# Two transformer stacks in one launch: heads turned back through a score bank, and the order of work at both borders of the feed-forward stage

## The reference, cut to what matters

```python
def hybrid_layer(x, ...):                       # first block, twice
    proj = rmsnorm(x, norm_g) @ w_in            # 28 columns of 128
    y_a = conformer_conv(a_u, a_v, ...) * silu(a_z)       # 31 taps
    y_b = short_gated_conv(b_b, b_c, b_x, ...) * silu(b_z)
    y_c = window_gqa(c_q, c_k, c_v, swa_sink) * silu(c_z)      # "gqa"
    y_d = neighborhood_attn(d_q, d_k, d_v, na_rpb) * silu(d_z) # "na"
    return x + concat(y_a, y_b, y_c, y_d) @ w_out

def second_block(x, ...):                       # second block, layers l = 0, 1
    proj = rmsnorm(h, attn_norm[l]) @ w_in[l]
    ret = silu(rg) * rmsnorm(retention_chunkwise(rq, rk, rv), ret_norm[l])
    dif = rmsnorm(diff_attention(dq, dk, dv, lam), diff_norm[l]) * (1 - lam_init)
    h = h + concat(ret, dif) @ w_out[l]
    u = rmsnorm(h, ffn_norm[l])
    h = h + (silu(u @ w_gate[l]) * (u @ w_up[l])) @ w_down[l]  # hidden width 2816
```

## Time and profile before

| what | value |
|---|---|
| median of 3 runs | 3571.68 us (3569.9 to 3572.59) |
| the profiled execution | 3570.65 us |
| its span | 3568.0 us |
| mean granted clock of TensorE | 0.988 of full speed |
| busy: TensorE, VectorE, POOL, ScalarE | 96, 55, 38, 28% of the span |
| bytes from and to HBM | 196.94 MB read, 41.68 MB written |

### The profile page before, as it was taken

The page is one execution under the profiler, slowest core; times in us unless marked ns, Lnnn a source line. Parts: engine busy times, 40 slices in busy tenths (PEclk is TensorE's granted clock), DMA queues, the critical chain, the costliest instruction groups (busy, mean ns, idle before and its releaser), DMA issues.

```text
span 3568.0 us, 41967 instructions
## 1 busy us (share of the span) xinstructions
PE 3417.0 (96%) x16504; PEld 2760.4 (77%) x16504; DVE 1960.6 (55%) x2939; ACT 993.6 (28%) x1863; POOL 1353.7 (38%) x592
## 2 busy tenths in 40 slices
PE   8999999999999999898999999999998989999997
PEld 7877778877778888567888888888875778888886
DVE  6668635668636333778656542331447776555324
ACT  2220342130243000554333330110026443333002
POOL 4324214324303433104655634543230255654443
PEclk9999999999999999999999999999999999999998
DMA  4112103112101111102222252211110122223322
GB/s 149 42 48 58 56 19 89 42 30 75 62 13 42 47 42 42 42 7 100 80 86 83 85 192 82 59 48 52 36 60 7 55 94 83 82 84 130 132 81 76
DMA packets 72812, 240.24 MB, mean 67 GB/s; under 512 B 21952, under 2 KB 22336, under 8 KB 66240
## 3 DMA queue, kind: packets, MB, share of 16 engines
q1 hardware_dynamic: 50112, 205.54, 17.2%
q10 hardware_dynamic: 22528, 32.31, 2.8%
HBM read 196.94 MB, written 41.68 MB: 67 GB/s over the span
## 4 chain that ended last, share of the span: by engine, by line
PE 84%; DVE 11%; ACT 2%; issue 2%; DMA 0%; DVEq 0%; ACTq 0%
PE ps L715 48%; PE ps L1102 23%; PE ps L844 3%; DVE st L1876 3%; PE ps L827 2%; PE ps L780 2%; PE ps L798 2%; DVE space_hi L1720 1%; DVE in_lo L1590 1%; DVE st L1596 1%; DVE xt L1578 1%; PE ps L855 1%; ACT st L1221 1%; PE ps L737 1%; DVE sl_r L2194 0%
## 5 line engine op out<-in xcount | busy, mean ns | idle before, releaser
L606 POOL TENSOR_TENSOR w_hi<-w_raw,ones_r 128x1024 fp32r<-128x1024 f32 x182 | 361.8, 1988 | 1775.4 <-PE ps L715 1758.9
L1102 PE MATMUL ps<-sl_r,sl_r 128*128 128x512 f32 x3696 | 843.7, 391 | 22.9 <-issue 22.9
L1102 PEld LDWEIGHTS ps<-sl_r,sl_r 128*128 128x128 f32 x3696 | 696.8, 189 | 168.7 <-issue 23.7
L715 PE MATMUL ps<-in_hi,w_hi 128*128 128x512 f32 x2176 | 696.1, 401 | 37.8 <-DVE in_lo L1590 16.2
L715 PE MATMUL ps<-in_hi,w_lo 128*128 128x512 f32 x2176 | 680.3, 394 | 0.0
L715 PE MATMUL ps<-in_lo,w_hi 128*128 128x512 f32 x2176 | 678.8, 393 | 0.0
L610 POOL TENSOR_TENSOR w_lo<-w_raw,w_hi 128x1024 fp32r<-128x1024 f32 x182 | 505.9, 2780 | 14.3
L715 PEld LDWEIGHTS ps<-in_hi,w_hi 128*128 128x128 f32 x2176 | 394.6, 189 | 143.3 <-issue 56.2
L715 PEld LDWEIGHTS ps<-in_lo,w_hi 128*128 128x128 f32 x2176 | 408.1, 189 | 90.5 <-issue 4.4
L715 PEld LDWEIGHTS ps<-in_hi,w_lo 128*128 128x128 f32 x2176 | 406.5, 189 | 91.9 <-issue 5.8
L715 PE MATMUL ps<-sl_r,w_hi 128*128 128x512 f32 x1408 | 378.7, 391 | 4.7 <-DVE sl_r L2236 4.7
(11 more groups left out here) (206 smaller groups left out, 3423.2 us busy)
## 6 DMA issues: line engine op xcount, KB each, us to landing
w_raw<-w_in SPq DMA_DIRECT2D x184, 512.0 KB, 3.5
raw_pair<-w_ffn SPq DMA_DIRECT2D x44, 1024.0 KB, 4.9
hid_kept<-sl SPq DMA_DIRECT2D x44, 512.0 KB, 2.6
sl<-hid_kept SPq DMA_DIRECT2D x44, 512.0 KB, 7.5
x_put_away<-xt SPq DMA_DIRECT2D x16, 512.0 KB, 7.8
xt<-x_put_away SPq DMA_DIRECT2D x16, 512.0 KB, 6.1
xt<-x_in ACTq DMA_DIRECT2D x8, 512.0 KB, 7.7
space_lo<-c_alibi ACTq DMA_DIRECT2D x2, 2048.0 KB, 7.6
```

The lines of the kernel that those rows point to most:

```text
L606: pool.tensor_tensor(w_hi[:, j, :], w_raw[:, j, :], ones[:, 0:1].broadcast_to([P, KC * P]), ALU.mult).then_inc(pool_own, 1)
L715: last = pe.matmul(ps[:, 2 * j + h, :], w[:, w_slot, (w_k + k) * P:(w_k + k + 1) * P], part[:, k0 + k, h * HALF:(h + 1) * HALF], start=(k ...
L1102: last = pe.matmul(ps[:, to[name], :], ring(sl_r, p, wp[w])[:, k * P:(k + 1) * P], half_of(sl_r, xp[x], k), start=(name in ("P1", "P5") an ...
```

## The change

**Heads.** In "gqa" and "na" the heads are turned back into bank 4, a score bank. The turn waits for the bias of all scores so far in place of bank 6, and the next scores wait for the finish. In "na", VectorE scales the heads ahead of the scores of its step, and ScalarE makes exponentials two steps behind the unit, between its two group copies.

**Border from the projection.** T2 and T3 are built in other banks, so P1 and P5 of pair 0 wait for the low part (T2, 1). The low parts of pair 0's plain weights go from VectorE to POOL (`rest_of_first`), the weights are rounded a step or two earlier on ScalarE, and the first `carry` stands ahead of the last chunk's work.

**Border to the down projection.** The last pair's gate is made in banks 5 and 6, so product 40 waits for the gate before it, and all low parts 1 to 7 are made ahead of the last `hidden`.

```diff
         def op_bank(op, i):
-            return {"T1": (4, 5, 6, 7), "T2": (6, 5, 6, 5), "T3": (7, 4, 7, 4)}[op][i]
+            return {"T1": (4, 5, 6, 7), "T2": (4, 6, 4, 3), "T3": (5, 7, 5, 1)}[op][i]
...
+        def gate_banks(p):
+
+            return (5, 6) if p == HC - 1 else (0, 1)
...
+            def rest_of_first(l, i):
+
+                raw = pair_raw(0)
+                hi, lo, source = ((sl_r[:, RING[0][0], :], sl_r[:, RING[0][4], :], raw[:, HALF:3 * HALF]),
+                                  (ring(sl_r, 0, (1, 0)), ring(sl_r, 0, (1, 1)), raw[:, 3 * HALF:4 * HALF]))[i]
+                pool.wait_ge(pair_hi.handle, pair_hi.at(1, l, rounded_count(0, 2 + i)))
+                pool.tensor_tensor(lo, source, hi.bitcast(F32), ALU.subtract).then_inc(pair_lo.handle, 1)
...
                         sums(l, 0)
+                        rest_of_first(l, 0)
                         sums_lo(l, 0)
+                        rest_of_first(l, 1)
...
+                    if state["back"]:
+                        pe.wait_ge(mixed_out.handle, mixed_out.at(stack, l, state["back"]))
+                        state["back"] = None
...
                     pe.wait_ge(headed.handle, headed.at(stack, l, r0 + n + 1))
-                    bank_6_free()
+                    if kind == "dif":
+                        bank_6_free()
+                        state["free"] = (mixed_out, r0 + n + 1)
+                    else:
+
+                        pe.wait_ge(biased.handle, biased.at(stack, l, p0 + state["p"]))
+                        state["back"] = r0 + n + 1
                     for c in range(4 * width // P):
-                        last = pe.transpose(ps[:, 6, c * P:(c + 1) * P],
+                        last = pe.transpose(ps[:, 6 if kind == "dif" else 4, c * P:(c + 1) * P],
...
-                    to = {"P1": a, "P5": 4 if p else 7, "P6": a, "P2": 0, "P7": a, "P3": 1, "P4": d}
+                    b, c = gate_banks(p)
+                    to = {"P1": a, "P5": 4 if p else 7, "P6": a, "P2": b, "P7": a, "P3": c, "P4": d}
...
-                            pe.wait_ge(op_lo.handle, op_lo.at(1, l, LO_ORDER.index(("T2", 2)) + 1))
+                            pe.wait_ge(op_lo.handle, op_lo.at(1, l, LO_ORDER.index(("T2", 1)) + 1))
...
-                pe.wait_ge(joined.handle, joined.at(1, l, 3 * HC))
+                pe.wait_ge(joined.handle, joined.at(1, l, 3 * (HC - 1)))
...
+                    if kind == "na" and 2 <= u < len(units) + 2:
+                        exps(u - 2)
                     if kind != "dif" and 3 <= u < len(units) + 3:
                         groups(u - 3, 1)
-                    if 1 <= u < len(units) + 1:
+                    if kind != "na" and 1 <= u < len(units) + 1:
                         exps(u - 1)
...
                     if op == "T3":
-                        last = (("T1", 3), ("T1", 0), ("T3", 0), ("T3", 1))[i]
-                        act.wait_ge(op_lo.handle, op_lo.at(1, l, LO_ORDER.index(last) + 1))
+                        last = (("T1", 1), ("T1", 3), ("T2", 0), None)[i]
+                        if last:
+                            act.wait_ge(op_lo.handle, op_lo.at(1, l, LO_ORDER.index(last) + 1))
...
-                    if p >= 2 and i == 3:
+                    if p == 0 and i == 2:
+                        act.wait_ge(op_lo.handle, op_lo.at(1, l, LO_ORDER.index(("T3", 3)) + 1))
+                    if p == HC - 1 and i == 2:
+
+                        act.wait_ge(gated.handle, gated.at(1, l, p))
+                    elif p >= 2 and i == 3:
...
                         for i in range(3):
                             x_hi("B21", i)
+                        carry(0, 0)
...
                         if c == 3:
                             put_half("T3", 0)
-                            put_half("T3", 1)
                     else:
                         squares(c)
+                        if c == 4:
+                            put_half("T3", 1)
...
-                    if c == 5:
-                        for i in (2, 3, 0):
+                    if c in (4, 5):
+                        for i in ((2, 3), (0, 1))[c - 4]:
                             pair_rounded(0, i)
-                    if c == 6:
-                        pair_rounded(0, 1)
-                carry(0, 0)
...
+                    if kind == "na" and heads_step(kind, 0) <= u <= heads_step(kind, NB - 1) and u % 4 == 3:
+                        heads(u // 4 - 1)
                     if u < len(units) and kind != "dif":
                         scores(u - u % 2, u % 2)
...
-                        if u == heads_step(kind, n):
+                        if kind != "na" and u == heads_step(kind, n):
                             heads(n)
...
-                    if c == KC - 2:
-                        pair_rest(0)
...
-                hidden_lo(1)
-                hidden_lo(2)
+                for i in range(1, 8):
+                    hidden_lo(i)
                 hidden(HC - 1)
-                for i in range(3, 8):
-                    hidden_lo(i)
```

More of the change, by code:

```diff
@@ L765, in attention @@
                 units = [(n, t) for n in range(NB) for t in range(4)]
-                state = {"p": 0, "g": 0, "free": None}
+                state = {"p": 0, "g": 0, "free": None, "back": None}
                 where = {}
@@ L1470, in carry @@
                         act.wait_ge(joined.handle, joined.at(1, l, 3 * p))
-                    if p >= 2 and i == 3:
+                    if p == 0 and i == 2:
[3 more added lines that the diff above has]
+                    elif p >= 2 and i == 3:
                         act.wait_ge(gated.handle, gated.at(1, l, p - 1))
-                    to, of = ((ps[:, 0, :], a), (half[:, :], 4 if p else 7), (ps[:, 1, :], a), (ps[:, d, :], a))[i]
+                    b, c = gate_banks(p)
+                    to, of = ((ps[:, b, :], a), (half[:, :], 4 if p else 7), (ps[:, c, :], a), (ps[:, d, :], a))[i]
                     act.activation(to, ps[:, of, :], ACT.Copy).then_inc(carried.handle, 1)
@@ L2197, in pair_rest @@
                 def pair_rest(p):
+                    if p == 1:
+                        dve.wait_ge(pair_lo.handle, pair_lo.at(1, l, 2))
                     raw = pair_raw(p)
@@ L2211, in join @@
                     dve.wait_ge(pair_done.handle, pair_done.at(1, l, 7 * p + 6))
-                    dve.tensor_tensor(ps[:, 1, :], ps[:, 1, :], half[:, :], ALU.add).then_inc(joined.handle, 1)
+                    dve.tensor_tensor(ps[:, c, :], ps[:, c, :], half[:, :], ALU.add).then_inc(joined.handle, 1)
                     dve.wait_ge(joined.handle, joined.at(1, l, 3 * p + 2))
@@ L2215, in join @@
                         dve.wait_ge(fac_ready.handle, fac_ready.at(1, l, 2))
-                    dve.tensor_tensor(sl[:, G_SLOT, :], flat(ps, 0, 2), rfac[:, :], ALU.mult).then_inc(joined.handle, 1)
+                    dve.tensor_tensor(sl[:, G_SLOT, :], flat(ps, b, 2), rfac[:, :], ALU.mult).then_inc(joined.handle, 1)
                 def hidden(p):
```

3 lines of the change are left out of this document (1 added, 2 removed).

## The result

The changed kernel takes **3523.7 us** (median of 4 runs, 3523.2 to 3526.7) against 3571.7: ratio 0.9868, interval 0.9857 to 0.988. Forecast were 3549.9 with a range of 3522 to 3563. The direction and the range held; the gain is 47.9 us where 21.8 were forecast. The profiled execution took 3526.67, 3.0 above the median; its span is 3524.8.

A forecast was written before the change was run, and what follows sets the result against it. TensorE bounds the kernel, with matmuls in flight for 96% of the span; only its idle stretches and lower-clock matmuls can be won. -11.4 - 14.8 - 7.4 + 12.8 = -20.8 from 3570.65 gives 3549.9 us, range 3522 to 3563.

The forecast's parts named there:

- the collision at the border from the projection: Before the spread of root and diagonals: POOL and VectorE alternate, spread 4.4 us later; +6.4 a layer, +12.8 in all.
- walk of the four queues: Border from the projection, up to the spread: followed with the rows' durations; POOL's L650 starts at 1675.5, before at 1681.30.
- the first rival: Border from the projection: no collision, POOL too late or VectorE keeps its turn; -11.0 in place of +12.8, 3526; chance 0.22.
- gqa: Heads turned back in attention "gqa": seven turns at 0.83 us each, some 5.7 a layer, -11.4 for both.
- na: Heads turned back in attention "na" and the two reorderings: -7.4 us a layer, -14.8 in all.
- late exponentials: In "na", an exponential ends only a step before its transposes: +0.2 us in four steps.
- The border to the down projection: Product 40 no longer stops at its fourth chunk, product 41 waits 0.4 us for the gate: -3.7 a layer, -7.4.
- second rival: The convolution swallows the gain of "gqa", TensorE waiting behind it: +11.4 us, so 3561; chance 0.12.

The follow-up runs named there:

- the benches: Kernels of their own without the computation: one POOL operation of 2.4 us is let go into chains of VectorE operations; in one chain it took 8.14 us.

## Why the prediction was wrong

**The step that failed** is the collision at the border from the projection: "Five operations of POOL (2.4, 2.4, 2.4, 1.2, 1.2) alternate with five of VectorE (0.6 each)". Its walk of the four queues up to POOL's L650 was right within 0.5 us, and that the two shut each other out was right too. Wrong was that they always take turns. In the rows that it rested on the earlier trace rows VectorE is just behind a stop: L1596 at 1645.98 follows three operations of 0.75 that start 0.79 apart, where they start 0.67 apart in a run, and the first L2204 at 1660.07 starts 0.04 behind the end of its forerunner. In the change VectorE had run ten or more operations without a stop when POOL came, and POOL was kept out. (The exclusion itself is in the change too: its L2239, 1024 wide, takes 1.22 us alone and up to 3.34 beside POOL, and the benches show turns up to the sixth operation. That POOL always has its turn behind VectorE's next operation is what the 8.14 us of the bench and the 2.5 us wait in the change contradict.) The term was +12.8 and measured -13.1 (matched matmuls), 15.8 by undoing it, a miss of 25.9. That the whole forecast was off by nearly the same, 26.2, is partly luck: the other terms gave 2.9 more than forecast, 6.5 went back, most of it at the lower clock, and the median lies 3.0 under the profiled execution. The outcome is the first rival, 0.22, whose 3526 is 2.3 us from the result. It named "VectorE keeps its turn" as a possibility, but what it weighed was only ScalarE's queue being 3 us slower, which it wasn't.

**Had the turns come**, the price was oversized. With the collision brought back the border's measure is 54.9 to 58.8 (three kernels, two layers) against 54.8 and 55.2 before: between 0.3 earlier and 3.6 later a layer, where 6.4 were summed. Three operations of POOL (in one layer of one kernel four), not five, fit between T4's four; the short sums fell beside root and diagonals.

**"gqa"**: 6.8 a layer for 5.7, and the sum hides two misses. The waits of the turns are all gone, but the seven turns of a layer gave 5.0, some 0.7 each, not 0.83. The other 1.8 were in no term. Before, TensorE waited 1.5 us for an evacuation behind the convolution's last taps, one of which took 2.80 because POOL's L606 ran beside it; in the change POOL starts 1 us before the last tap ends, stretches none (two taps in 2.61), and that wait is gone, in both layers:

```profile
324.81 4.12 DVE L1876 SCALAR_TENSOR_TENSOR st<-st,cur 128x1023 f32<-128x1023 f32 x2
...
330.33 0.70 PE L715 MATMUL ps<-in_hi,w_hi 128*128 128x512 f32 x2 [1.51 <-DVE st L1572]
```

```profile
310.61 0.70 PE L729 MATMUL ps<-in_hi,w_hi 128*128 128x512 f32 x2 [1.56 <-DVE st L1603]
...
320.19 2.61 DVE L1909 SCALAR_TENSOR_TENSOR st<-st,cur 128x1023 f32<-128x1023 f32 x2
```

(first before, then the change). The clock adds nothing: before, 3.4 us at the lower clock (granted 0.5 of full speed) stood near 302 and 855, after the change there is none there, but the 1.6 us that this gives TensorE go at once into the new wait of 1.56 in the second fence.

**"na"**: 7.4 and 7.7 for 7.4. Turn 0 waits 1.43 for its bias, the costliest of six such waits (4.4 in both layers), and late exponentials cost 2.8 in six waits (forecast 0.2 in four steps a layer, 1.6). The sum held all the same, so something else gave more than forecast; what did was not taken apart.

**The border to the down projection**: 3.9 for 3.7, with seven low parts from 2057.85, the gate behind them and product 41 starting 0.3 us late (forecast 0.4).

**The later convolution** swallowed nothing of the turns' gain (second rival): matched matmuls are 5.0 us a layer earlier on both sides of the waits near 302 and 855. It took only what the clock had given, by the new wait above.

## What to carry to other kernels

Where VectorE and POOL both run operations with two inputs in SBUF, look at how many operations VectorE issues without a stop before POOL arrives. In a short run (up to five or six here) POOL gets every other turn, and four operations of 0.6 us become 9 (9.23, 9.07 and 9.05 in three kernels); in a long one POOL waits (7.31 us for two operations of 2.4) and VectorE keeps its pace (2.49 for the four). So on a critical stretch of VectorE leave no needless wait or link in the run, not even one of 0.1 us. And when a forecast rests on a rule seen in a few rows, ask in what state the engine was in those rows.

## What the runs showed that was not expected

- VectorE and POOL take turns for the first operations of a run of VectorE, and not at all from the seventh on: 2.65 us against 5.73 for the same POOL operation let go one operation later (twelve of 512). A met wait (4.53), an operation with one input and one that reads PSUM (5.13 both) don't end the run; a wait that stops VectorE does (2.72), one of 0.1 us in the kernel too. Whether the sixth itself gives way was yes in the bench (2.65, 3.25) and no in one place of one kernel, in both layers (L662 x2 in 8.63). What counts so was not tried.
- One wait of 0.1 us a layer cost 15 us of a kernel (3538.8 against 3523.7), and one memset of 0.07 us a layer with its wait 20 us; the same memset nine operations earlier cost nothing that can be measured (3527.0, border 48.6).
- The profiled executions of kernels that are the same up to the first border reach it between 1622.9 and 1633.0 us.
